# Expert-value stage of a transformer block: activations of two value slabs per operation, and their gelu fetched by one load

## The reference, cut to what matters

```
u_sel = u[expert]
v_sel = v[expert]
a = jax.nn.gelu(jnp.einsum('cd,chkd->chk', xc, u_sel), approximate=False) * g
return jnp.einsum('chk,chkd->cd', a, v_sel)
```

## Time and profile before

| | us |
|---|---|
| median of 3 runs | 1685.6 (1685.28 to 1688.26) |
| the profiled execution | 1683.52 |
| its span | 1681.3 |

### The profile page before, as it was taken

One profiled execution on the slowest core, in us unless ns is written; L12 is line 12 of the kernel. 1 busy time (PEld: TensorE's weight loads), 2 busy tenths in 40 slices (PEclk: granted clock), 3 DMA queues, 4 the chain that ended last, 5 costly groups with the idle time before them and its releaser, 6 DMA issues. The chain is left out here.

```text
span 1681.3 us, 26829 instructions
## 1 busy us (share of the span) xinstructions
PE 1633.2 (97%) x9808; PEld 1509.0 (90%) x9808; DVE 1341.1 (80%) x2856; ACT 735.2 (44%) x1288; POOL 455.5 (27%) x314
## 2 busy tenths in 40 slices
PE   5999999999799999999999999999999999999996
PEld 4897776678688899999999999999999999999996
DVE  4534455646568899999999989768899999899898
ACT  3314444443253344667666754444333333333331
POOL 0000000000001023333133342333554555457540
PEclk9999999999899999999999999999999999999998
DMA  4461111023234478899899999999999999999991
GB/s 147 121 198 57 42 50 39 13 84 95 85 99 148 134 251 302 275 353 327 276 311 346 331 347 320 368 406 362 405 404 407 407 409 407 407 407 406 407 404 77
DMA packets 185441, 438.47 MB, mean 261 GB/s; under 512 B 17832, under 2 KB 102000, under 8 KB 182880
## 3 DMA queue, kind: packets, MB, share of 16 engines
q1 hardware_dynamic: 73872, 227.43, 37.1%
q0 software_dynamic: 44080, 161.06, 26.0%
q10 hardware_dynamic: 67360, 48.28, 8.7%
HBM read 380.57 MB, written 56.13 MB: 260 GB/s over the span
## 5 line engine op out<-in xcount | busy, mean ns | idle before, releaser
L469 PE MATMUL psS<-hT_lo,hi 128*128 128x368 f32 (+2 forms) x1464 | 503.1, 344 | 4.6 <-DVE hT_lo L1033 3.9
L460 DVE TENSOR_TENSOR lo<-raw,hi 128x1024 fp32r<-128x1024 f32 x323 | 394.4, 1222 | 132.8 <-ACT hi L456 124.8
L470 PE MATMUL psS<-hT_hi,lo 128*128 128x368 f32 (+2 forms) x1464 | 495.0, 338 | 0.0
L471 PE MATMUL psS<-hT_hi,hi 128*128 128x368 f32 (+2 forms) x1464 | 492.8, 337 | 0.0
L456 ACT ACTIVATE hi<-raw 128x1024 fp32r<-128x1024 f32 x323 | 339.8, 1053 | 160.5 <-PE psS L471 104.0
L578 POOL DMA_INDIRECT gat<-in_u_rows,idx x144 | 216.4, 1503 | 395.9 <-DVE gat L1207 214.6
L469 PEld LDWEIGHTS psS<-hT_lo,hi 128*128 128x128 f32 x1464 | 275.2, 188 | 28.7 <-issue 15.8
L471 PEld LDWEIGHTS psS<-hT_hi,hi 128*128 128x128 f32 x1464 | 275.5, 188 | 12.4
L470 PEld LDWEIGHTS psS<-hT_hi,lo 128*128 128x128 f32 x1464 | 275.2, 188 | 10.1
L578 POOL DMA_INDIRECT gat<-in_v_exp,idx x144 | 222.4, 1544 | 225.5 <-DVE gat L1207 141.6
L773 ACT ACTIVATE act_hi<-act_t 128x368 fp32r<-128x368 f32 x128 | 65.6, 513 | 275.9 <-DVE act_t L1258 265.0
(11 more groups left out here) (314 smaller groups left out, 2667.4 us busy)
## 6 DMA issues: line engine op xcount, KB each, us to landing
raw<-in_u_exp SPq DMA_DIRECT2D x128, 512.0 KB
raw<-in_v_exp SPq DMA_DIRECT2D x128, 512.0 KB
gelu_dram<-gelu ACTq DMA_DIRECT2D x128, 184.0 KB
gates_dram<-gates ACTq DMA_DIRECT2D x92, 256.0 KB
gel_in<-gelu_dram SPq DMA_DIRECT2D x128, 184.0 KB
raw<-in_w_merge SPq DMA_DIRECT2D x24, 512.0 KB
gate_even<-gates_dram SPq DMA_DIRECT2D x8, 1472.0 KB
gate_odd<-gates_dram SPq DMA_DIRECT2D x8, 1472.0 KB
```

The source lines that it names most:

```text
L460: nc.vector.tensor_tensor(lo[:, n % RING, :], raw[:, n % RING, :], hi[:, n % RING, :].bitcast(F32), ALU.subtract).then_inc(lo_done, 1)
L469: nc.tensor.matmul(out_ap, w_h, x_l, start=start, stop=False)
L470: nc.tensor.matmul(out_ap, w_l, x_h, start=False, stop=False)
L471: return nc.tensor.matmul(out_ap, w_h, x_h, start=False, stop=stop)
```

## The change

Value slabs are prepared in pairs (v even, v + 1). `gelu_dram` is laid out as [64, 128, 2, 368], so that the two slabs' gelu lie side by side for each partition; ACT stores them one by one as before, and SP fetches a pair with one load at even v, after both stores. DVE makes `act_t` of a pair in one operation of 736 columns, in odd steps, and `act_lo` of a pair in one, in even steps; ACT makes `act_hi` of a pair in one, in odd steps. The rings keep four places. The planner's figure for this work falls from 1.02 to 0.92 a step, which moves items.

```diff
     for s in range(NKEYS - AHEAD, 2 * NKEYS - AHEAD):
-        vector[s] += 1.02
+        vector[s] += 0.92
...
-        gelu_dram = nc.dram_tensor("gelu_dram", [NKEYS, P, DENSE], F32).ap()
+        gelu_dram = nc.dram_tensor("gelu_dram", [NKEYS // 2, P, 2, DENSE], F32).ap()
...
-                if 0 <= v < NKEYS:
-                    sp.wait_ge(gelu_out[v % RING], 16 * (v // RING + 1))
+                if 0 <= v < NKEYS and v % 2 == 0:
+                    for w in (v, v + 1):
+                        sp.wait_ge(gelu_out[w % RING], 16 * (w // RING + 1))
                     if v >= RING:
-                        sp.wait_ge(act_done, v - RING + 1)
-                    sp.dma_start(gel_in[:, v % RING, :], gelu_dram[v]).then_inc(gel_in_s[v % RING], 16)
+                        sp.wait_ge(act_done, v - RING + 2)
+                    sp.dma_start(gel_in[:, v % RING:v % RING + 2, :], gelu_dram[v // 2]).then_inc(gel_in_s[v // 2 % 2], 16)
...
-                if v + AHEAD >= 0 and v + AHEAD < NKEYS:
+                if 0 <= v + AHEAD < NKEYS and (v + AHEAD) % 2 == 0:
                     w = v + AHEAD
-                    act.wait_ge(act_done, w + 1)
+                    act.wait_ge(act_done, w + 2)
                     if w >= RING:
-                        act.wait_ge(slab_used, FIRST_V + w - RING + 1)
-                    nc.scalar.activation(act_hi[:, w % RING, :], act_t[:, w % RING, :], ACT.Copy).then_inc(ahi_done, 1)
+                        act.wait_ge(slab_used, FIRST_V + w - RING + 2)
+                    nc.scalar.activation(act_hi[:, w % RING:w % RING + 2, :], act_t[:, w % RING:w % RING + 2, :],
+                                         ACT.Copy).then_inc(ahi_done, 2)
...
-                    act.dma_start(gelu_dram[s], gelu[:, s % RING, :]).then_inc(gelu_out[s % RING], 16)
+                    act.dma_start(gelu_dram[s // 2][:, s % 2, :], gelu[:, s % RING, :]).then_inc(gelu_out[s % RING], 16)
...
-                if 0 <= v + AHEAD < NKEYS:
+                if 0 <= v + AHEAD < NKEYS and (v + AHEAD) % 2 == 0:
                     w = v + AHEAD
-                    g = w // VGROUP
+                    g, two = w // VGROUP, slice(w % RING, w % RING + 2)
...
-                    V.tensor_tensor(act_t[:, w % RING, :].rearrange("p (q t) -> p q t", t=STORED),
-                                    gel_in[:, w % RING, :].rearrange("p (q t) -> p q t", t=STORED),
-                                    gate_in[g % 2][:, :, at:at + STORED], ALU.mult).then_inc(act_done, 1)
-                if 0 <= v + 2 < NKEYS:
+                    V.tensor_tensor(act_t[:, two, :].rearrange("p s (q t) -> p s q t", t=STORED),
+                                    gel_in[:, two, :].rearrange("p s (q t) -> p s q t", t=STORED),
+                                    gate_in[g % 2][:, :, at:at + 2 * STORED].rearrange("p q (s t) -> p s q t", t=STORED),
+                                    ALU.mult).then_inc(act_done, 2)
+                if 0 <= v + 2 < NKEYS and v % 2 == 0:
                     w = v + 2
-                    dve.wait_ge(ahi_done, w + 1)
+                    two = slice(w % RING, w % RING + 2)
+                    dve.wait_ge(ahi_done, w + 2)
                     if w >= RING:
-                        dve.wait_ge(slab_used, FIRST_V + w - RING + 1)
-                    V.tensor_tensor(act_lo[:, w % RING, :], act_t[:, w % RING, :], act_hi[:, w % RING, :].bitcast(F32),
-                                    ALU.subtract).then_inc(alo_done, 1)
+                        dve.wait_ge(slab_used, FIRST_V + w - RING + 2)
+                    V.tensor_tensor(act_lo[:, two, :], act_t[:, two, :], act_hi[:, two, :].bitcast(F32),
+                                    ALU.subtract).then_inc(alo_done, 2)
```

More of the change, by code:

```diff
@@ L414, in build @@
         gates_out = [sem(f"gates_out{r}") for r in range(2)]
-        gel_in_s, gate_in_s = [sem(f"gel_in{r}") for r in range(RING)], [sem(f"gate_in{r}") for r in range(2)]
+        gel_in_s, gate_in_s = [sem(f"gel_in{r}") for r in range(2)], [sem(f"gate_in{r}") for r in range(2)]
         act_done, ahi_done, alo_done = sem("act_done"), sem("ahi_done"), sem("alo_done")
@@ L1250, in _ @@
                         dve.wait_ge(gates_out[0], 16 * STORE_PARTS * stores_of[0])
-                    dve.wait_ge(gel_in_s[w % RING], 16 * (w // RING + 1))
+                    dve.wait_ge(gel_in_s[w // 2 % 2], 16 * (w // RING + 1))
                     if w % VGROUP == 0:
@@ L1254, in _ @@
                     if w >= RING:
-                        dve.wait_ge(ahi_done, w - RING + 1)
-                        dve.wait_ge(alo_done, w - RING + 1)
+                        dve.wait_ge(ahi_done, w - RING + 2)
+                        dve.wait_ge(alo_done, w - RING + 2)
                     at = w % VGROUP * STORED
-                    V.tensor_tensor(act_t[:, w % RING, :].rearrange("p (q t) -> p q t", t=STORED),
-                                    gel_in[:, w % RING, :].rearrange("p (q t) -> p q t", t=STORED),
-                                    gate_in[g % 2][:, :, at:at + STORED], ALU.mult).then_inc(act_done, 1)
-                if 0 <= v + 2 < NKEYS:
+                    V.tensor_tensor(act_t[:, two, :].rearrange("p s (q t) -> p s q t", t=STORED),
[3 more added lines that the diff above has]
+                if 0 <= v + 2 < NKEYS and v % 2 == 0:
                     w = v + 2
-                    dve.wait_ge(ahi_done, w + 1)
+                    two = slice(w % RING, w % RING + 2)
+                    dve.wait_ge(ahi_done, w + 2)
                     if w >= RING:
-                        dve.wait_ge(slab_used, FIRST_V + w - RING + 1)
-                    V.tensor_tensor(act_lo[:, w % RING, :], act_t[:, w % RING, :], act_hi[:, w % RING, :].bitcast(F32),
-                                    ALU.subtract).then_inc(alo_done, 1)
+                        dve.wait_ge(slab_used, FIRST_V + w - RING + 2)
+                    V.tensor_tensor(act_lo[:, two, :], act_t[:, two, :], act_hi[:, two, :].bitcast(F32),
+                                    ALU.subtract).then_inc(alo_done, 2)
                 at_position(FIRST_U + s)
```

## The result

The changed kernel takes 1689.2 us (median of 20 runs, 1686.2 to 1690.1), the kernel before 1686.1 (20 runs beside it). The ratio is 1.0017, interval 1.0010 to 1.0024: 2.9 us slower (1.7 to 4.0), where 2.2 us were forecast.

What follows compares the result with a forecast made beforehand. DMA traffic was taken to set the value slabs' pace, by a hair over PE. Terms -2.8, +5.1, +0.5, -0.8 and +0.2 sum to +2.2 us, giving 1687.8 us; range 1683.0 to 1692.8.

Steps and rivals of the forecast that it cites:

- DMA traffic sets the pace of the value slabs: Value slabs: DMA at 4.10 us a slab against PE's 4.04; PE loses 7.3 us, the most to be regained.
- Items moved: Four more items between steps 148 and 240, at 1.27 us of DMA each where DMA sets the pace: +5.1 us.
- Fewer packets: Paired gelu loads halve data and semaphore packets, 0.03 us a slab from v = 20 to 112: -2.8 us.
- gelu ahead of the gates: Gelu load leaves before the gate load, so the stall at 1228 us shrinks: -0.8 us, ends 0 and -3.3.
- longer load: The pair's gelu load is twice as long, so gel_in lands later: +0.2 us.
- The price of a packet: DMA queues: time is 6.8 ns for each packet plus 0.038 ns for each byte.
- Lead: Early value slabs lose about 0.7 of 4.3 us lead as act_hi of a pair waits longer: +0.5, ends 0 and 1.3.
- Long round: Two items in even steps, v = 48 to 94: 8.23 us a pair against PE's 8.08; priced 0, else 3.6 us.
- the slower rival: Value slabs: the longer two-step round adds 3.6 us, +5.8 in all, 1691.4 us; chance 0.37.
- DVE and ACT time: Merged operations save DVE 0.14 us a pair, 9 us over the stage, all beside PE and DMA: 0.
- The forecast of 2650 to 2665 matmuls: PE's matmuls in the same window of the value slabs, 1184 to 1640 us, against 2671 before.
- the short ones at pairs: DVE waits for gel_in under 1 us, expected at pairs instead of just after gate loads.

Runs made afterwards that it cites:

- load_pair_only: The kernel before with only the paired gelu load and its DRAM layout, operations and items as before; 1683.7 us, ratio 0.9988 to the kernel before.
- gelu_before_gates: The kernel before, but where gates are loaded SP issues that slab's gelu load ahead of them; 1686.3 us, ratio 1.0003 to the kernel before.
- light_after: The changed kernel, but from the third gate load on each brings 6 of 23 parts; 1679.5 us, ratio 0.9967 to the kernel before.
- the two repairs: The changed kernel with each step pair's greater item count in the odd step (1.0004), or with ACT's hi ahead of act_hi (1.0007); ratios to the kernel before.
- hi_first_more_early: The changed kernel with ACT's hi ahead of act_hi and the planner's figure at 1.12; 1680.5 us, ratio 0.9964 to the kernel before.
- items_only: The kernel before with only the planner's figure lowered from 1.02 to 0.92, so items move; 1692.4 us, ratio 1.0033 to the kernel before.

## Why the prediction was right, point by point

The time, 1689.2 us, lies in the range (1683.0 to 1692.8), 1.4 above the value; in ratios +2.9 us against +2.2. What was said of the main cause held: items moved onto a full DMA cost more than the pairs give. That the value is so close is partly luck. The load was worth 1.4 us less than counted, and the paired operations with their round together came out 1.2 us better than the +0.5 taken for them (2.9 - 5.6 + 2.0 = -0.7), and these two nearly cancel.

- **DMA traffic sets the pace of the value slabs, 7.3 us are there to be had.** Shown: with 15.6 MB less, PE loses nothing and the kernel gains 7.1 us (0.9958).
- **Items moved, +5.1.** Measured +5.6 us (3.7 to 7.4) alone, 0.2 with DMA relieved. Right in size and in kind: the planner was told that DVE had room, and spent the room on the resource that had none.
- **Fewer packets, -2.8; gelu ahead of the gates, -0.8; longer load, +0.2.** Together -3.4, measured -2.0 for the paired load (load_pair_only). The price of a packet holds on the new trace: 25697 x 6.8 ns + 99.38 MB x 0.038 ns a byte is 3951 us, the row says 54.3% of 16 x 456, 3962. The -0.8 for the gates is not confirmed: gelu_before_gates gives +0.5 (-1.0 to +2.0), which leaves room for it and rules out the -3.3 of its end. The argument against it stood in the prediction (raw of the next slab stays behind the same bytes).
- **Lead, +0.5: not confirmed, perhaps wrong in sign.** By the medians the paired operations give 1.9 us on top of the paired load (3.9 against 2.0), where a small loss was taken as net; but the intervals of the two overlap. Half of the slabs have act_lo a step earlier, and a late raw can then stall PE on every other slab only: that this is the gain is argued, not shown.
- **Long round, 0: the step that failed.** It was put as "if DMA did not already hold the pace there. It does (...), so I forecast 0 for it". The period was right to 0.03 us (8.26 against 8.23); the conclusion wasn't. DMA was full, and yet it was not DMA that these rounds waited for: in 21 of 23 of them ACT had no wait for raw. The old round takes 7.48 us and wins back time between two gate loads, which the prediction had noted as a doubt; the new one can't, and where both items of a step add to `y_row` it was longer still, 8.53. The 23 rounds took 8.40 us each on average, more than either bound (8.23 and 8.30). With DMA relieved, light_after still loses 2.2 us. In the changed kernel it is worth about 2 us by the two repairs (give or take 2), in the slower rival's direction but, by the medians, not its full 3.6.
- **DVE and ACT time, 0.** The freed 9 us of DVE are there (1341.1 to 1332.3 us over the span); no run shows that they pay.

The forecast of 2650 to 2665 matmuls in the window was missed by two (2648); some nine of them are due to the clock, below. That the gel_in wait behind the gates would go held; the short ones at pairs that were expected in its place are not in the list either. ACT's wait for raw did not stay "about as long as before": it grew from 44.3 to 62.6 us.

## What to carry to other kernels

Before a planner's cost for one engine is lowered, ask which resource the work that it then moves will need: here DVE was made lighter, the planner moved gathers, and DMA, full to 1.03, paid for them. When two slabs' operations are merged, look at what is queued behind the longer one on each engine: act_hi of two slabs stood ahead of the hi that DVE waited for next, and swapping them cost nothing that a run shows. And where two bounds lie within a few per cent of each other (here 8.23 and 8.30 us against PE's 8.08), zero is not a safe price for the second: a round that could win back time between two bursts of loading no longer can.

## What the runs showed of the hardware

A stall of PE can cost more than itself. In the changed kernel PE issued nothing new from 1370.0 to 1371.96 us, and then its matmuls, at first 0.17 us apart, started 0.31 us apart, eleven of them; the granted clock (the last column but two) falls to half, that is from 2.4 to 1.2 GHz:

```profile
1368.00:1371.00 3.00, 2.17 (x13) 1.86 (x11) 1.47 (x4) 1.06 (x1) 0.94 (x1) 1.00 1.03 411
1371.00:1373.00 2.00, 1.04 (x6) 1.07 (x7) 2.00 (x3) 1.06 (x1) 0.00 (x0) 1.00 1.01 402
1373.00:1375.00 2.00, 2.00 (x9) 2.00 (x8) 2.00 (x4) 0.00 (x0) 1.68 (x1) 0.50 1.04 416
1375.00:1377.00 2.00, 2.00 (x10) 2.00 (x9) 2.00 (x3) 0.79 (x2) 1.67 (x1) 0.65 1.02 392
```

Eleven matmuls at 0.31 us instead of 0.17 are 1.5 us, on top of the stall's 1.9. gelu_before_gates shows the same after a stall of 2.3 us that ends at 1397.7 us (granted clock 0.55, then 0.67), and hi_first_more_early after one of 2.5 us in the u slabs (0.57). items_only does not after one of 2.2 us before 1233.3 us (1.00), nor does the changed kernel after one of 1.7 us before 1272.3 us:

```profile
1231.00:1233.00 2.00, 0.21 (x2) 0.00 (x0) 0.86 (x2) 0.28 (x1) 0.00 (x0) 1.00 1.05 411
1233.00:1235.00 2.00, 1.72 (x10) 1.75 (x11) 1.54 (x4) 1.29 (x2) 0.45 (x1) 1.00 1.03 403
```

What decides between them is open. The timed difference is not made by such falls: the granted clock of the changed kernel's 20 executions averages 0.9931, that of the executions of before, chip by chip, 0.9930 to 0.9935. In the kernel before, no stall of the value slabs was over 1 us, and the clock stayed at 1.00 in them.
